# Last mixer in pairs of heads: two-head queries on row halves of the array, means on GpSimd, output blocks between transposes

## The chip, the cores and the metric

One core of a Trainium2 chip runs the whole program, one launch. The metric is the time on the device in microseconds; a time of the kernel is the median of its runs.

## The reference, cut to what matters

Two transformer stacks of two layers each, on 256 latent and 256 context tokens of width 1024, follow each other. The change lies in the fourth and last mixer, an mLSTM with 8 heads (64 query and key columns, 128 value columns per head), run in both directions (r = 0, 1) over the latents, from a state that the context left:

```python
def body(carry, inp):
    c_mat, n_vec, m = carry
    qc, kc, vc, ic, fc = inp
    b = jnp.cumsum(fc, axis=-1)
    logd = b[..., :, None] - b[..., None, :] + ic[..., None, :]
    logd = jnp.where(tri, logd, -jnp.inf)
    inter = b + m[..., None]
    m_t = jnp.maximum(inter, jnp.max(logd, axis=-1))
    s = jnp.einsum('bhtd,bhsd->bhts', qc, kc) * jnp.exp(logd - m_t[..., None])
    w_inter = jnp.exp(inter - m_t)
    num = einsum('bhts,bhsv->bhtv', s, vc) + w_inter[..., None] * einsum('bhtd,bhdv->bhtv', qc, c_mat)
    den = jnp.sum(s, axis=-1) + w_inter * einsum('bhtd,bhd->bht', qc, n_vec)
    out = num / jnp.maximum(jnp.abs(den), jnp.exp(-m_t))[..., None]

def _mlstm_readout(h, o, norm_w, w_out):      # h: sum over both directions
    h = h * lax.rsqrt(jnp.mean(h * h, axis=-1, keepdims=True) + EPS)
    return (jax.nn.sigmoid(o) * (h.reshape(...) * norm_w)) @ w_out
```

After it come the norm, the gate and the residual, and the last MLP (1024 to 4096 to 1024).

## The kernel before

Each engine has its own program, written out by hand in order; they meet on semaphores. Weights stream from HBM by SyncE into a ring of four raw tiles (`raw`). A walk over the blocks (`walk.take`) splits each block of 128x1024 into a high part by ScalarE (L1747, `split`) and a low part by VectorE (L2482) or, where `low_by_pool` is set, by GpSimd (L3486), up to five blocks ahead. TensorE then makes every product of the projections from three fp32r matmuls (high by high, high by low, low by high: L764, L770, L771; `mm3`). Products inside the mixer (`mm`, L774) are plain fp32, each of them two TensorE instructions in the trace. Eight PSUM banks are handed out in order of return (`ps.take`, `ps.give`).

Between the blocks the walk also drops units of the modulation product: multiply-adds of `ada` tiles on VectorE (L2507), so many per block by the table `RATE`. The last piece of a chunk of gates closes with a high copy (ScalarE), a low remainder `accl` (VectorE, L2550), two matmuls with ones (TensorE) and two operations that make the gate rows `G` (L2564, L2566). `walk.ensure` forces what is still open.

The last mixer (`mlstm` in all four engines' programs) goes over 16 steps, `steps = (h, r)`, both directions of head 0, then of head 1 and so on. Step j of TensorE: `maxima` of the next step (selects the row of maxima, into `mD`), for r = 0 `matches(h)` (keys by queries, both blocks of keys, into `mS`), one `gate_part` or `key_part` (12 fp32r matmuls of a projection that fills the step), then `back` of the step before: two matmuls of the queries with the state `m_C` and three of the weighted scores `m_S` with the values `m_vl`. The keys of heads 2p and 2p+1 lie in rows 0 to 63 and 64 to 127 of one tile; the queries have one tile per head, of which the other 64 rows are zero (GpSimd memsets), so each product runs over 128 rows. VectorE: `front` (decay arguments, L3297), `weigh` (scores by decays, L3307), `back` (adds up numerator and denominator, L3318), `over_den` (three small operations, L3327 to L3331), `head_sum` (both directions added, L3337, twice), and for each pair of heads `means` (L3344), `normed` (L3350), `gated` (L3362, twice), `gated_low` (L3370). ScalarE: the exponentials (`front`, L2364, twice), `back` (state part scaled, `m_T`, L2373, twice), `over_den` (L2381), `head_squares` (L1779), `o_out`, `gated_high` (L2397). GpSimd: `root` (power -1/2, L3699), `gate` (L3704) and the low parts of the weight blocks. Decay, score and state tiles are chosen by the direction r, two of each.

Each pair of heads is turned by four transposes (`normed` of TensorE, L1624) at steps 8 and 12, and after the loop. Then `proj_last` multiplies by `ml_w_out`: four blocks (all 1024 rows) for output columns 0 to 511 of both token tiles, `walk.ensure((3, 2))` for the gates of this layer, then four more blocks for columns 512 to 1023, tile 2 and then tile 3. In `transition` each tile is squared, gated (`gated_out`, L2681), added to the residual, normed and transposed for the MLP.

## Time and profile before

| | us |
|---|---|
| median of 3 runs | 1907.23 (1904.70 to 1908.61) |
| the profiled execution, its own time | 1903.66 |
| its span, first to last instruction | 1901.8 |
| mean granted TensorE clock | 0.997 |
| TensorE busy | 1862.8 (98%) |
| VectorE busy | 1374.1 (72%) |
| ScalarE busy | 926.8 (49%) |
| GpSimd busy | 248.4 (13%) |
| chain that ended last | TensorE 85%, VectorE 7%, ScalarE 3% |

TensorE carries nearly the whole span, so over most of it only its own instructions count; where it is idle, the chain of waits passes to another engine. The times of the trace are counted from the start of the span. Matmuls overlap in the trace, so what one costs is read from start to start.

### The profile page before, as it was taken

What the parts mean: (1) busy time and instruction counts of PE and PEld (TensorE: products, weight loads), DVE (VectorE), ACT (ScalarE), POOL (GpSimd) and SP (SyncE); (2) the same over time, 40 slices, a digit from 0 to 9 for tenths busy, and PEclk for the clock granted to TensorE, in tenths of its full rate; (3) what the DMA queues carried; (4) which work ended last, traced back from release to release, by engine and by line L of the source; (5) the groups of instructions that cost most, each with busy time, mean ns of one, the idle gap of its engine ahead of it and who ended that gap; (6) DMA issues with size and microseconds to landing.
All of it is one profiled execution on the core that took longest, in us unless ns stands there. A gap on an engine that the chain in (4) does not pass through costs nothing.

```text
span 1901.8 us, 27100 instructions
## 1 busy us (share of the span) xinstructions
PE 1862.8 (98%) x10121; PEld 1578.6 (83%) x10121; DVE 1374.1 (72%) x2135; ACT 926.8 (49%) x1593; POOL 248.4 (13%) x331
## 2 busy tenths in 40 slices
PE   7999999999999999999999999999999999989998
PEld 3878888888888788899998889888888878878997
DVE  5898778878766565789987766777665477676765
ACT  3666463424144473666552236433424354656654
POOL 1111011111111202201110001010110020321000
PEclk9999999999999999999999999999999999999999
DMA  9544255656652641588854433555554255237763
GB/s 317 153 126 144 78 177 178 209 176 192 189 188 59 200 130 53 175 270 281 268 179 145 139 104 112 177 178 169 174 168 141 60 183 169 86 108 248 224 191 112
DMA packets 192433, 315.31 MB, mean 166 GB/s; under 512 B 16229, under 2 KB 113840, under 8 KB 192304
## 3 DMA queue, kind: packets, MB, share of 16 engines
q1 hardware_dynamic: 163024, 210.09, 34.4%
q0 software_dynamic: 29280, 103.51, 18.0%
q8 instruction: 81, 1.33, 0.3%
q14 instruction: 48, 0.39, 0.1%
HBM read 312.50 MB, written 1.05 MB: 165 GB/s over the span
## 4 chain that ended last, share of the span: by engine, by line
PE 85%; DVE 7%; ACT 3%; issue 3%; DMA 1%; POOL 1%; DVEq 0%; SPq 0%; POOLq 0%; ACTq 0%
PE bank L764 26%; PE bank L771 24%; PE bank L770 24%; PE bank L774 6%; PE bank L769 2%; PE bank L767 2%; DVE acc L2507 1%; DVE w L2482 1%; PE bank L826 1%; PE bank L850 1%; ACT junk L1779 1%; POOL st L3558 1%; DMA raw<-in_ada_w 1%; DVE X L2626 1%; DVE HL L2611 0%
## 5 line engine op out<-in xcount | busy, mean ns | idle before, releaser
L1747 ACT ACTIVATE w<-raw 128x1024 fp32r<-128x1024 f32 (+2 forms) x386 | 398.3, 1040 | 527.7 <-PE bank L771 464.7
L2482 DVE TENSOR_TENSOR w<-raw,w 128x1024 fp32r<-128x1024 f32 (+3 forms) x368 | 438.8, 1201 | 223.0 <-ACT w L1747 222.5
L764 PE MATMUL bank<-HH,w 128*128 128x256 f32 (+1 forms) x1552 | 508.5, 328 | 3.4 <-DVE HH L2609 2.0
L770 PE MATMUL bank<-HL,w 128*128 128x512 f32 (+1 forms) x1232 | 412.5, 335 | 0.0
L771 PE MATMUL bank<-HH,w 128*128 128x512 f32 (+1 forms) x1232 | 412.4, 335 | 0.0
L2507 DVE SCALAR_TENSOR_TENSOR acc<-ada,sc,acc 128x512 f32<-128x512 f32 x518 | 362.6, 748 | 2.3
L764 PEld LDWEIGHTS bank<-HH,w 128*128 128x128 f32 x1552 | 291.4, 188 | 30.3 <-issue 4.4
L764 PE MATMUL bank<-w,UH 128*128 128x512 f32 x768 | 300.6, 391 | 0.0
L771 PE MATMUL bank<-w,UL 128*128 128x512 f32 x768 | 299.1, 389 | 0.0
L770 PE MATMUL bank<-w,UH 128*128 128x512 f32 x768 | 298.9, 389 | 0.0
L771 PEld LDWEIGHTS bank<-HH,w 128*128 128x128 f32 x1232 | 230.5, 187 | 26.1
L770 PEld LDWEIGHTS bank<-HL,w 128*128 128x128 f32 x1232 | 230.7, 187 | 25.7 <-issue 0.2
L771 PEld LDWEIGHTS bank<-w,UL 128*128 128x128 f32 x768 | 144.2, 188 | 30.3
L770 PEld LDWEIGHTS bank<-w,UH 128*128 128x128 f32 x768 | 144.2, 188 | 29.2
L764 PEld LDWEIGHTS bank<-w,UH 128*128 128x128 f32 x768 | 144.2, 188 | 29.1
L3495 POOL DMA_DIRECT2D ada<-in_mod_w x96 | 69.4, 724 | 535.2 <-DVE acc L2507 535.2
L764 PE MATMUL bank<-w,HH 128*128 128x512 f32 (+2 forms) x336 | 128.2, 382 | 2.0 <-issue 2.0
L771 PE MATMUL bank<-w,HL 128*128 128x512 f32 (+2 forms) x336 | 126.7, 377 | 0.0
L770 PE MATMUL bank<-w,HH 128*128 128x512 f32 (+2 forms) x336 | 126.5, 376 | 0.0
L2784 DVE TENSOR_TENSOR UL<-tp,UH 128x256 fp32r<-128x256 f32 (+1 forms) x128 | 69.9, 557 | 76.4 <-ACT UH L1938 75.9
L3495 POOL DMA_DIRECT2D ada<-in_ada_w x80 | 58.0, 726 | 344.8 <-DVE acc L2507 344.8
L1930 ACT ACTIVATE ta<-bank 128x256 f32<-128x256 f32 (+1 forms) x128 | 62.5, 488 | 81.5 <-PE bank L771 78.4
(366 smaller groups left out, 2515.9 us busy)
## 6 DMA issues: line engine op xcount, KB each, us to landing
raw<-in_mlp_w SPq DMA_DIRECT2D x256, 512.0 KB, 4.4
ada<-in_mod_w POOLq DMA_DIRECT2D x96, 512.0 KB, 4.7
ada<-in_ada_w POOLq DMA_DIRECT2D x80, 512.0 KB, 4.6
raw<-in_ml_w_qkvo SPq DMA_DIRECT2D x28, 512.0 KB, 3.7
raw<-in_conv_w_in SPq DMA_DIRECT2D x24, 512.0 KB, 3.6
raw<-in_ada_w SPq DMA_DIRECT2D x12, 512.0 KB, 6.2
raw<-in_mla_w_o SPq DMA_DIRECT2D x8, 512.0 KB, 3.9
raw<-in_gla_w_v SPq DMA_DIRECT2D x8, 512.0 KB, 3.7
```

The lines of the kernel that those rows point to most:

```text
L764: pe.matmul(o, sh, mh, start=start, stop=False, skip_group_check=True)
L767: pe.matmul(o, sl, mh, start=False, stop=False, skip_group_check=True)
L769: return pe.matmul(o, sh, ml, start=False, stop=stop, skip_group_check=True)
L770: pe.matmul(o, sh, ml, start=False, stop=False, skip_group_check=True)
L771: return pe.matmul(o, sl, mh, start=False, stop=stop, skip_group_check=True)
L774: return pe.matmul(o, st, mv, start=start, stop=stop, skip_group_check=True)
L1747: act.activation(k.halves(n)[0], k.raw[(NDIRECT + n) % NRAW][:, 0:m], ACT.Copy).then_inc(*k.w_hi.up("w hi", n))
L1930: act.activation(t1[:, 0:N], b[:, 0:N], ACT.Relu).then_inc(*b.emptied())
L2482: dve.tensor_tensor(low, k.raw[(NDIRECT + n) % NRAW][:, 0:m], high.bitcast(F32), ALU.subtract).then_inc(*k.w_lo.up("w lo", n))
L2507: i = dve.scalar_tensor_tensor(out=o, in0=k.ada[m % NADA][:, q, :], scalar=cc, in1=o, op0=ALU.mult, op1=ALU.add)
L2784: dve.tensor_tensor(UL[:, n, 0:N], t2[:, 0:N], UH[:, n, 0:N].bitcast(F32), ALU.subtract).then_inc(*k.u_lo.up("u lo", li, q, n))
L3495: pool.dma_start(k.ada[m % NADA][:], src).then_inc(*k.ada_in[m % NADA].up("ada in", m, by=16))
```

## The change

Steps of the loop are now pairs: `(0,0) (1,0) (0,1) (1,1) (2,0) ...`. The query tile holds a pair of heads (four tiles, no zeros, two memsets and half the copies gone). `matches` runs once per pair and `recalled` (the queries with the state) once per pair and direction, with 64-row operands that alternate between the two row halves of the array and write two banks. Decay, score and state tiles are chosen by the head's parity. ScalarE scales both heads' state parts at the odd steps. Sums, squares and transposes of a pair stand one to two steps later. The mean moves from VectorE to GpSimd, just ahead of the power. `ml_w_out` is streamed as rows 0 to 511 for both column halves, then rows 512 to 1023. Its first four blocks come right after the loop, the transposes of heads 4, 5 and of 6, 7 stand ahead of the third and the fourth of them, and the last four blocks close tile 2 and then tile 3 (`gated_out` of columns 0 to 511 now per tile). `RATE` of the last layer's first part goes from 0.8 to 0.9.

```diff
-    yield from tokw(A["ml_w_out_2"][0], 0, D, 0, D)
+    for r0 in (0, D // 2):
+        yield from tokw(A["ml_w_out_2"][0], r0, D // 2, 0, D)
-RATE = [(1.2, 1.05), (0.65, 0.45), (0.4, 0.8), (0.8, 0.35)]
+RATE = [(1.2, 1.05), (0.65, 0.45), (0.4, 0.8), (0.9, 0.35)]
...
-        def matches(h):
...
-                p = mm(b[:, s * 256:s * 256 + 256], k.mkT[:, pr, s * 128:s * 128 + 128], k.mqT[:, h, :])
+        def matches(pr):
+            bs = [ps.take("mS", 2 * pr + i) for i in range(2)]
...
+            for s in range(2):
+                for i, b in enumerate(bs):
+                    w.wait_ge(*b.before())
+                    c = i * 64
+                    p = mm(b[:, s * 256:s * 256 + 256], k.mkT[c:c + 64, pr, s * 128:s * 128 + 128], k.mqT[c:c + 64, pr, :])
...
+        def recalled(pr, r):
+            bs = [ps.take("mx", 2 * pr + i, r) for i in range(2)]
+            w.wait_ge(*ps.of("mC", r, pr // 2).is_empty())
+            for t in range(2):
+                for i, b in enumerate(bs):
...
+                    p = mm(b[:, t * 129:t * 129 + 129], k.mqT[c:c + 64, pr, t * 128:t * 128 + 128], k.mC[c:c + 64, r, pr, :])
...
         def back(h, r):
-            b1, b2 = ps.take("mn", h, r), ps.take("mx", h, r)
+            if h % 2 == 0:
+                recalled(h // 2, r)
+            b1 = ps.take("mn", h, r)
...
-        steps = [(h, r) for h in range(8) for r in range(2)]
+        steps = [(2 * pr + i, r) for pr in range(4) for r in range(2) for i in range(2)]
...
-            if j in (8, 12):
-                turned = normed((j - 8) // 4)
+            if j in (10, 14):
+                turned = normed((j - 10) // 4)
...
-        proj_last(("y", 3, 2), (k.mOH, k.mOL), [2, 3], o_ready, 2, among={2: lambda: ps.give(normed(3))})
+        for nh in range(2):
+            bs = [ps.take("y", 3, 2, nh, t) for t in (2, 3)]
+            for kk in range(2):
+                if nh * 2 + kk == 2:
+                    ps.give(normed(2))
+                if nh * 2 + kk == 3:
+                    ps.give(normed(3))
+                n = walk.take()
...
+        walk.ensure((3, 2))
+        slots = walk.take4()
+        for t in (2, 3):
+            for nh in range(2):
+                for kk in (2, 3):
+                    p = part(kk, nh, t, slots[nh * 2 + kk - 2])
...
-            act.activation(k.mqT[0:64, 2 * n, :], b[0:64, 0:256], ACT.Copy, scale=0.125)
-            act.activation(k.mqT[64:128, 2 * n + 1, :], b[64:128, 0:256], ACT.Copy, scale=0.125).then_inc(*b.emptied())
+            act.activation(k.mqT[:, n, :], b[:, 0:256], ACT.Copy, scale=0.125).then_inc(*b.emptied())
...
+            if c % 2:
+                back(j - 1)
+                back(j)
...
         def root(fp):
...
-            w.wait_ge(*at("mean", "mz", fp))
+            w.wait_ge(*at("mz sq", fp * 2 + 1))
+            pool.tensor_scalar(s[1], s[0], 1.0 / 128, EPS, ALU.mult, ALU.add).then_inc(*own.up())
+            w.wait_ge(*own.last())
```

How it moves instructions. Line numbers in the rows of the changed kernel are its own. TensorE, in the loop, before (`m_C,m_qT`: queries with state; `m_vl,m_S`: scores with values; `m_M,Gh`: maxima; `m_qT,m_kT`: matches; the row after them is the filling projection):

```order
L774 MATMUL bank<-m_C,m_qT 128x129 x2
L774 MATMUL bank<-m_vl,m_S 128x129 x3
L774 MATMUL bank<-m_M,Gh 128x256
L774 MATMUL bank<-m_qT,m_kT 128x256 x2
L764 MATMUL bank<-HH,w 128x256
```

The same place now:

```order
L775 MATMUL bank<-m_C,m_qT 128x129 x4
L775 MATMUL bank<-m_vl,m_S 128x129 x3
L775 MATMUL bank<-m_M,Gh 128x256
L775 MATMUL bank<-m_qT,m_kT 128x256 x4
L765 MATMUL bank<-HH,w 128x256
```

The queries stand there four at a time, in every second step, the matches four at a time, in every fourth; there are as many of them in all as before.

ScalarE, four steps late in the loop, before (`m_D`: exponentials; `m_T`: state parts; `Y<-Y`: division by the denominator; `junk,Y<-Y`: squares; `w<-raw`: high part of a weight block):

```order
L2364 ACTIVATE m_D<-m_D,m_cols 128x256 x2
L2373 ACTIVATE m_T<-bank,m_cols 128x129 x2
L2381 ACTIVATE Y<-Y 128x128 x2
L1779 ACTIVATE junk,Y<-Y 128x128 x2
L2364 ACTIVATE m_D<-m_D,m_cols 128x256 x2
L2373 ACTIVATE m_T<-bank,m_cols 128x129 x2
L2393 ACTIVATE m_so<-bank 128x256
L1747 ACTIVATE w<-raw 128x1024
```

and now:

```order
L2408 ACTIVATE m_D<-m_D,m_cols 128x256 x2
L2438 ACTIVATE m_so<-bank 128x256
L2418 ACTIVATE m_T<-bank,m_cols 128x129 x4
L2426 ACTIVATE Y<-Y 128x128 x2
L2408 ACTIVATE m_D<-m_D,m_cols 128x256 x2
L1823 ACTIVATE junk,Y<-Y 128x128 x2
L1791 ACTIVATE w<-raw 128x1024
L2408 ACTIVATE m_D<-m_D,m_cols 128x256 x2
```

The state parts of two steps follow each other, and the step between has none.

VectorE, behind the loop, before (`HL<-tp,HH`: low part of the mixer's last heads; `accl`: low remainder of the gate sums):

```order
L3370 TENSOR_TENSOR HL<-tp,HH 128x2x256
L2482 TENSOR_TENSOR w<-raw,w 128x1024 x4
L2550 TENSOR_TENSOR accl<-acc,Gh 128x512
L2564 TENSOR_TENSOR G<-bank,gb 128x512
L2566 SCALAR_TENSOR_TENSOR G<-G,gb 128x512
```

and now:

```order
L3425 TENSOR_TENSOR HL<-tp,HH 128x2x256
L2538 TENSOR_TENSOR w<-raw,w 128x1024 x4
L2620 TENSOR_TENSOR G<-bank,gb 128x512
L2622 SCALAR_TENSOR_TENSOR G<-G,gb 128x512
L2538 TENSOR_TENSOR w<-raw,w 128x1024
```

`accl` is gone from here; it now stands ahead of the loop.

## Rows read from the trace of the kernel before

**Rows 1.** Windows: busy us (x instructions), granted clock, DMA share, GB/s.
```profile
1621.70:1643.60 21.90, 21.90 (x179) 21.48 (x179) 13.06 (x34) 16.29 (x45) 8.10 (x6) 1.00 0.30 97
1643.60:1675.80 32.20, 26.55 (x206) 24.57 (x204) 22.84 (x54) 22.37 (x66) 11.46 (x7) 1.00 0.20 66
1675.80:1697.40 21.60, 16.82 (x80) 14.23 (x81) 16.13 (x23) 11.09 (x26) 7.07 (x6) 0.92 0.29 88
1697.40:1708.70 11.30, 11.11 (x50) 8.86 (x48) 7.84 (x13) 4.88 (x10) 1.12 (x2) 1.00 0.52 162
```

**Rows 2.** Waits of TensorE, 1621 to 1725 us: total, times, longest.
```profile
PE bank L1624 <- DVE Y L3350: 6.2, 3, 2.6
PE bank L774 <- DVE accl L2550: 2.2, 1, 2.2
```

**Rows 3.** Timeline of TensorE in one step: start, us, instructions.
```profile
1621.76 0.61 PE L774 MATMUL bank<-m_C,m_qT 128*128 128x129 f32 x4
1622.20 0.83 PE L774 MATMUL bank<-m_vl,m_S 128*128 128x129 f32 x6
...
1622.99 1.03 PE L774 MATMUL bank<-m_qT,m_kT 128*128 128x256 f32 x4
1623.67 0.47 PE L764 MATMUL bank<-HH,w 128*128 128x256 f32 x1
```

**Rows 4.** Windows of tile g_s in an earlier mixer; last: the first one's group.
```profile
732.62:734.55 1.93, 1.92 (x16) 1.46 (x16) 0.04 (x1) 0.00 (x0) 1.00 0.00 0
734.55:736.47 1.92, 1.92 (x10) 1.44 (x8) 0.00 (x0) 0.00 (x0) 1.00 0.00 0
...
L774 PE MATMUL bank<-Y,g_s 64*128 64x256 f32 x16 | 2.0, 389 | 0.0
```

**Rows 5.** Timeline of VectorE in the loop; last two: groups, 1643.6 to 1675.8.
```profile
1641.33 0.69 DVE L3297 SCALAR_TENSOR_TENSOR m_D<-bank,m_msk 128x512 f32<-128x512 f32 x1
...
1644.09 1.45 DVE L3337 SCALAR_TENSOR_TENSOR Y<-Y 128x128 f32<-128x128 f32 x2
...
1652.35 0.62 DVE L3337 SCALAR_TENSOR_TENSOR Y<-Y 128x128 f32<-128x128 f32 x2 [0.35 <-ACT Y L2381]
...
1658.11 0.69 DVE L3297 SCALAR_TENSOR_TENSOR m_D<-bank,m_msk 128x512 f32<-128x512 f32 x1
...
L3318 DVE TENSOR_TENSOR Y<-bank,m_T 128x258 f32<-128x258 f32 x9 | 3.8, 426 | 8.7 <-ACT m_T L2373 8.7
...
L1779 ACT ACTIVATE junk<-Y 128x128 bf16<-128x128 f32 x8 | 2.5, 310 | 4.6 <-DVE Y L3337 4.5
```

**Rows 6.** Timeline of GpSimd in the loop.
```profile
1643.14 1.99 POOL L3486 TENSOR_TENSOR w<-raw,w 128x1024 fp32r<-128x1024 f32 x1
...
1674.53 1.38 POOL L3699 TENSOR_TENSOR Y<-Y,minus_half 128x4 f32<-128x4 f32 x1 [5.75 <-DVE Y L3344]
...
1676.48 2.37 POOL L3486 TENSOR_TENSOR w<-raw,w 128x1024 fp32r<-128x1024 f32 x1
```

**Rows 7.** Timeline of VectorE behind the loop and in the transition.
```profile
1674.96 0.68 DVE L3307 TENSOR_TENSOR m_S<-bank,m_D 128x512 f32<-128x512 f32 x1
...
1675.90 3.10 DVE L3337 SCALAR_TENSOR_TENSOR Y<-Y 128x128 f32<-128x128 f32 x2
...
1689.20 0.88 DVE L3362 SCALAR_TENSOR_TENSOR tp<-bank,m_nwc,m_so 128x256 f32<-128x256 f32 x2 [1.69 <-PE bank L1624]
1690.78 0.69 DVE L3370 TENSOR_TENSOR HL<-tp,HH 128x512 fp32r<-128x512 f32 x1 [0.70 <-ACT HH L2397]
1691.80 4.63 DVE L2482 TENSOR_TENSOR w<-raw,w 128x1024 fp32r<-128x1024 f32 x4 [0.33 <-ACT w L1747]
1696.35 0.68 DVE L2550 TENSOR_TENSOR accl<-acc,Gh 128x512 fp32r<-128x512 f32 x1
...
1709.27 0.21 DVE L2588 TENSOR_SCALAR st<-ysq 128x1 f32<-128x1 f32 x1 [0.33 <-ACT junk L1779]
1709.40 0.68 DVE L2681 TENSOR_TENSOR Y<-bank,G 128x512 f32<-128x512 f32 x1
```

More of the change, by code:

```diff
@@ L1633, in mlstm @@
                 maxima(*steps[j + 1])
-            if r == 0:
-                matches(h)
-            else:
+            if j % 4 == 0:
+                matches(h // 2)
+            if r == 1:
                 ps.give(ps.of("mS", h))
@@ L1906, in transition @@
         walk.cut_next()
+        if (li, part) == (3, 2):
+            y_out(li, part)(0, 3)
         y_out(li, part)(1, 3)
@@ L2758, in transition @@
         walk.ensure((nli, 3 * which), (nli, 3 * which + 1))
+        if (li, part) == (3, 2):
+            gated_out(li, part, 0, 3)
         y_out(li, part)(1, 3)
@@ L3289, in mlstm, with front @@
         proj_feat(1, kt_out)
-        def front(h, r):
+        def front(j):
+            h, r = steps[j]
             b = ps.of("mD", h, r)
@@ L3339, in head_sum @@
             a.then_inc(*k.z_dve.up("head sum", h))
-        def means(fp):
-            w.wait_ge(*at("mz sq", fp * 2 + 1))
-            ms = [k.st_ml[:, a, :].rearrange("p (t h) -> p t h", t=2)[:, :, fp * 2:fp * 2 + 2] for a in range(2)]
-            dve.tensor_scalar(ms[1], ms[0], 1.0 / 128, EPS, ALU.mult, ALU.add).then_inc(*k.mean_in.up("mean", "mz", fp))
         def normed(fp):
@@ L3373, in mlstm @@
         walk.low_by_pool = True
-        steps = [(h, r) for h in range(8) for r in range(2)]
-        front(*steps[0])
-        for j, (h, r) in enumerate(steps):
+        steps = [(2 * pr + i, r) for pr in range(4) for r in range(2) for i in range(2)]
+        front(0)
+        for j in range(16):
+            done, c = j // 4 * 2 - 2, j % 4
             if j < 15:
-                front(*steps[j + 1])
+                front(j + 1)
             if j < 2 or j % 2 == 0:
                 walk.take()
-            weigh(h, r)
+            weigh(j)
             if j == 1:
@@ L3386, in mlstm @@
                 back(*steps[j - 1])
-            if h and r:
-                head_sum(h - 1)
-            if h and not r:
-                over_den(h - 1)
-            if j in (6, 10, 14):
-                means((j - 6) // 4)
-            if j in (7, 11, 15):
-                normed((j - 7) // 4)
-            if j in (9, 13):
-                gated((j - 9) // 4)
-            if j in (10, 14):
-                gated_low((j - 10) // 4)
-        walk.take()
+            if c == 3:
+                over_den(done + 2)
+            if done >= 0 and c == 0:
+                over_den(done + 1)
+            if done >= 0 and c in (1, 2):
+                head_sum(done + c - 1)
+            if j in (9, 13):
+                normed((j - 9) // 4)
+            if j in (11, 15):
+                gated((j - 11) // 4)
+            if j == 13:
+                gated_low(0)
         back(*steps[-1])
         over_den(7)
+        head_sum(6)
+        gated_low(1)
+        normed(2)
         head_sum(7)
+        walk.take()
         gated(2)
-        means(3)
         gated_low(2)
@@ L3409, in mlstm @@
         walk.low_by_pool = False
-        proj_last(3, 2, [2, 3])
+        for _ in range(4):
+            walk.take()
+        walk.ensure((3, 2))
+        walk.take4()
+        gated_out(3, 2, 0, 2)
     w.wait_ge(*at("ident"))
@@ L3707, in mlstm @@
         for j in range(16):
-            if j in (6, 10, 14):
-                root((j - 6) // 4)
-                gate((j - 6) // 4)
+            if j in (8, 12):
+                root((j - 8) // 4)
+                gate((j - 8) // 4)
             if j < 2 or j % 2 == 0:
                 walk.take()
-        walk.take()
+        root(2)
+        gate(2)
         gate(3)
         root(3)
+        walk.take()
         walk.low_by_pool = False
```

129 lines of the change are left out of this document (75 added, 54 removed).

## Prediction

> **What bounds the kernel now.** I read the page first: TensorE is busy for 98% of the span and holds 85% of the chain that ended last. So a change can win only where TensorE is idle, slow, or does work that falls away. The windows [rows 1] split the stretch that the change touches in four. In 1621.7 to 1643.6 (`back` of steps 0 to 7) TensorE is busy throughout: it is the bound. In 1643.6 to 1675.8 (up to the last `back`) it is busy 26.55 of 32.2 us. In 1675.8 to 1697.4 (the last filling product, the first half of the output product) it is busy 16.82 of 21.6 us, at a granted clock of 0.92. In 1697.4 to 1708.7 (the second half) it is full again. Idle sums to 5.65 + 4.78 = 10.4 us; the clock took 8% of 21.6 us, 1.7 us. The waits of TensorE [rows 2] name two causes: 6.2 us of three waits by the transposes for `normed` of VectorE, and 2.2 us of the gate's matmul for `accl`. The last two windows hold what can be had; all of it, with the work that falls away below, would be 14 us.
>
> **Row halves.** TensorE's pieces are read from start to start [rows 3]. The state part of one step is 1622.20 - 1621.76 = 0.44 us. Matches of one head are 1623.67 - 1622.99 = 0.68 us, and the matmul behind them shows 0.47 us where those that follow it show 0.28, so 0.87 us. Are two row halves really at work at once? An earlier mixer alternates 64-row products in the same way [rows 4]: 16 of them, all of the form 64*128 with 256 columns, lie within 1.93 us, and in the next 1.92 us only the 8 with 128 rows (the other two counted are tails). Eight slots, of 128 rows or of a pair, take the same time; if one is the 0.87 / 4 = 0.216 us of a match (the trace shows four instructions for a head), eight make 1.73 us, so 0.2 us goes with each change of shape, and 0.4 us with a visit there and back. The Trainium skill (TensorEngine Tiling (Array Packing), Key Properties) says that changing the tiling mode drains TensorE; the row agrees and gives the price. Now per pair of heads: matches before 2 x 0.87 = 1.74 us, after 0.87 + 0.4 = 1.27 us. State parts, per pair and direction: before 0.88, after 0.44 + 0.4 = 0.84 us. So four pairs save 4 x (0.47 + 0.08) = 2.2 us of TensorE's work, and where it is the bound (7 of 16 steps) 2.2 x 7/16, **1.0 us**.
>
> **The late loop.** Here the bound is VectorE's order of work with its round trips to ScalarE. Its first instruction of a step starts at 1641.33 and, four steps later, at 1658.11 [rows 5]: 16.8 us, where TensorE needs 12.5 to 13 us (21.9 us for seven steps, [rows 1], and 0.44 us of transposes). In each step VectorE waits for `m_T` before its `back`: 8.7 us in nine steps, 0.96 us each. The state part on ScalarE stands behind an exponential that itself waited for VectorE. In the changed order both state parts of a pair are made at the odd steps, so that at the even ones they are there: 2 x 0.96 us less. `head_sum` stands a step behind its ScalarE division: the 0.35 us that it waited, twice. The mean (0.14 us) is GpSimd's. Together 1.92 + 0.70 + 0.14 = 2.8 us. Then GpSimd: two `head_sum` operations take 0.62 us at 1652.35, and 1.45 us at 1644.09, where a low part on GpSimd runs from 1643.14 to 1645.13 [rows 5, 6]; they end just behind it. The same thing takes 3.10 us at 1675.90 [rows 7], under low part 1676.48 to 1678.85. The Trainium skill (GPSIMD Engine Reference, in its table and again among its limits) says that GpSimd shares its SBUF interfaces with VectorE, with contention when a VectorE instruction has two SBUF inputs; `head_sum` has, `back` and `weigh` read one from PSUM and keep their 0.43 and 0.68 us throughout, so the trace agrees. In the new order the mean, power and gate of a pair start half a step earlier against the `head_sum` that follows, but the queue is longer by the mean, so I let the 0.83 us go and put 0.7 us of such waits in again. Four steps come to 16.8 - 2.8 - 0.1 = 13.9 us, eight to 27.8 us where they took 32.2; I add 1.1 us for two places where I expect more: ScalarE makes `o_out` ahead of the state parts in one odd step of four, and `matches` of the last pair takes the bank that a state part just left. That is **3.3 us** less.
>
> **Behind the loop.** I measure from the end of the last `weigh` (1674.96 + 0.68 = 1675.65, [rows 7]) to the last matmul of the output, 1708.35 (the end of `accl`, 1697.03, and the 11.3 us of the last window): 32.7 us. After: the last `back` and filling product end by 2.1 us (a step of 21.9 / 7 = 3.1 us without maxima, state part and matches). The three output blocks that come ahead of the last transposes take 2.78 us each (11.11 us for four blocks, [rows 1]), with one set of transposes 0.44 us: TensorE reaches the last transposes at 10.9 us. VectorE's chain up to the last `head_sum`: two `back` (0.43 each), two sets of denominators (three small operations each, none longer than the 0.21 us of the one at 1709.27, [rows 7]: 0.6), `gated` 0.88, two `head_sum` (0.62), a low part 0.69, `normed` 0.68, and 0.7 us of round trips, 6.2 us in all. Behind it: squares (two of 0.31 us [rows 5] with their sums, 0.8), the mean, the power 1.38 [rows 6] and `normed` 0.68. The mean on GpSimd has no row: it lies between 0.14 us (what VectorE took) and 1.38 us (the power on the same four elements), and is nearest to the power, an operation of that engine and shape; I take 1.0 us; at either end what it costs is under 1 us. That is 10.9 us, and with a low part of 2.37 us on GpSimd beside it that holds up VectorE for part of its time, `normed` comes at 11.6 us, so transposes end at 12.1 us. From `gated` to the last low part were 1691.47 - 1689.20 = 2.3 us [rows 7]: 14.4 us. Now the gain: before, TensorE could not begin the second half until **four** low parts of weights (4.63 us) and `accl` (0.68 us) stood behind that point on VectorE. `accl` is ahead of the loop now, so only the first low part (0.2 + 1.2 us) is needed: 15.8 us. The other three come every 1.16 us, and TensorE takes 2.78 / 2 = 1.39 us for each half block, so they are hidden. Then 48 matmuls, 10.9 us (11.11 in [rows 1] with the gate's own): end at 26.7 us, **6.0 us** less, the lower clock's 1.7 us included, since no wait of 2.6 us is left in a row.
>
> **Transition.** `gated_out` of columns 0 to 511 of tile 3 (0.68 us) now lies in VectorE's order ahead of the last tile's mean, where before it idled 0.33 us [rows 7]: **0.35 us more**. It waits there for nothing later than its squares, but the tile's mean and gating are queued behind it.
>
> **At nothing:** the memsets and halved query copies lie beside full TensorE windows. So do the `ada` units that the rate 0.9 brings forward; if VectorE were late there, TensorE would wait. The stream of `ml_w_out` has the same blocks in another order; the DMA share in these windows is 0.2 to 0.52.
>
> **Sum:** -1.0 - 3.3 - 6.0 + 0.35 = -9.95 us, against the profiled execution's 1903.66 us: 1893.7 us. That execution lay 3.6 us under the median, so against 1907.2 us I predict 1897.3 us. Some 0.2% (3.8 us) is what a measurement of this kernel can tell from no change.
>
> **Rivals.** (1) *GpSimd holds VectorE* (slower). The longer GpSimd queue (mean, power, gate, then 2.37 us of low part) falls upon both `head_sum` pairs of each of three late pairs. For: rows 5 to 7 show it twice. Against: the one at 1652.35 was free, and in most steps GpSimd has nothing to do (11.46 of 32.2 us busy, [rows 1]). Price: up to 2.4 us per place, six places, 14.4 us: 4.5 us slower than before. It decides for slower when the added waits pass 9.9 us, that is at five of six places. Chance 0.04. (2) *Halves do not overlap* in this place: TensorE's pieces stay at 1.74 and 0.88 us and 12 visits x 0.4 us = 4.8 us come on top; against my sum that is 1.0 + 4.8 x 7/16 = 3.1 us in the early steps and about 0.6 us late, -6.2 us in all. Rows 4 speak against it. 0.08. (3) *The late loop keeps its pace*: the wait for `m_T` only moves to the odd steps, where two state parts and `o_out` stand ahead. -1.0 - 6.0 + 0.35 = -6.6 us. For: ScalarE was busy 22.37 of 32.2 us there [rows 1]. 0.16. (4) *The tail keeps its wait*, because something else stands last before the second half (the last pair's chain late by 4 to 5 us, through GpSimd's power); of the 6.0 us only 1 us of the clock's stays: -1.0 - 3.3 + 0.35 - 1.0 = -4.9 us. 0.12. (5) *Both 3 and 4*: -1.0 + 0.35 - 1.0 = -1.6 us, no change that can be told. 0.09. (6) *It does not do what it says*: the order of instructions shows the pairs, so this is only that `accl` is late all the same; it is within 4.
>
> The forecast has 0.51. Faster by over 0.2%: forecast, 2, 3 and 4, 0.87, less 0.02 for their low ends; within 0.2%: 0.11; slower: 0.04. The range: best case all idle and clock regained, 14 us less 0.35, is 1893.6 us; at the other end case 4 with its spread, 1904 us.
>
> **What would show it.** Right: TensorE's wait for `normed` at the transposes under 2 us in all instead of 6.2; no wait for `accl`; matches with 64-row operands, 8 in about 0.9 us; starts of VectorE's steps 14 us apart per four; the granted clock at 1.0 between the loop and the second half; `m_T` waits of VectorE in every second step only. Wrong: `head_sum` of 2 to 3 us under low parts on GpSimd; new waits of TensorE for ScalarE or for banks ahead of `matches`; a second half that starts over 18 us behind the last `weigh`; a loop where four steps still take over 16 us.

## The result, and the profile after

| | before | after |
|---|---|---|
| median, us | 1906.21 (1904.70 to 1908.61, 4 runs) | 1892.90 (1891.75 to 1893.16, 4 runs) |
| ratio | | 0.9928, 95% interval 0.9911 to 0.9945 |
| the profiled execution | 1903.66 | 1892.93 |
| its span | 1901.8 | 1891.1 |
| TensorE busy | 1862.8 | 1858.7 |
| VectorE busy | 1374.1 | 1370.1 |

The changed kernel is faster by 0.72%, 13.3 us between the medians and 10.7 us between the two profiled executions. The interval of the ratio stands for 10.5 to 17.0 us. The fourth run of before, made beside the changed kernel, moved its median from 1907.23 to 1906.21.

Where is it? I cut both traces at the same five marks of TensorE's program: the first product of `matches`, the first score product (`m_vl,m_S`) of the 8th and of the 16th `back`, the first product of the second half of the output projection, and the transposes of the last tile in the transition. The stretches are called **early**, **late**, **tail** and **second half** from here on. Windows, columns as in rows 1 (length, busy us of TensorE, its weight loads, VectorE, ScalarE and GpSimd with instructions, granted clock, DMA share, GB/s). Before:

```profile
1615.20:1644.11 28.91, 28.91 (x236) 28.39 (x235) 17.18 (x41) 20.46 (x54) 10.60 (x7) 1.00 0.34 106
1644.11:1676.31 32.20, 26.55 (x204) 24.57 (x203) 22.93 (x54) 21.91 (x64) 11.46 (x8) 1.00 0.20 66
1676.31:1697.42 21.11, 16.33 (x79) 13.72 (x77) 15.62 (x22) 11.11 (x26) 6.56 (x5) 0.92 0.29 91
1697.42:1714.02 16.60, 15.75 (x90) 13.28 (x89) 12.11 (x21) 7.78 (x16) 2.79 (x5) 1.00 0.46 142
```

The changed kernel:

```profile
1617.26:1645.41 28.15, 28.15 (x239) 25.75 (x239) 17.44 (x41) 20.08 (x54) 10.38 (x7) 1.00 0.29 92
1645.41:1670.69 25.28, 23.86 (x200) 21.62 (x199) 18.51 (x46) 20.00 (x60) 10.94 (x9) 1.00 0.27 85
1670.69:1687.59 16.90, 14.99 (x79) 11.97 (x77) 12.00 (x24) 9.27 (x25) 7.63 (x8) 1.00 0.20 62
1687.59:1704.48 16.89, 15.82 (x89) 13.36 (x89) 15.23 (x24) 10.79 (x22) 2.79 (x5) 1.00 0.60 189
```

Early -0.76, late -6.92, tail -4.21, second half +0.29: 98.82 us became 87.22, **11.6 us less**. Two differences lie outside and are not the change's. The first mark itself is 2.06 us later; 1.94 of that is there at 1574 us and 1.77 at the start of the first mixer, 78.76 us before against 80.53, in code that the change does not touch. The granted clock shows where it comes from: from 47.4 to 50.8 us it is 0.50 in the profile of the changed kernel (13 matmuls) and 1.00 in that of before (21 matmuls). In the 14 profiles of this study the first mark lies between 1615.2 and 1616.3 us in the four without such a stretch ahead of it, and between 1617.0 and 1618.6 in the ten with one or two. And from the last mark to the end it is 187.8 us before and 186.6 after, because before ran with a granted clock of 0.50 from 1718.0 to 1720.0. That differs from one execution to the next too: of the 14 profiles 7 have the long ending (187.6 to 188.2 us) and 7 the short one (186.6 to 186.7), and the last two experiments, equal in the stretch, differ in it.

Waits of TensorE in the changed kernel, 1617 to 1710 us, against [rows 2]:

```profile
PE bank L1635 <- DVE Y L3405: 2.4, 2, 1.3
PE bank L851 <- DVE Y L2655: 1.1, 2, 0.9
...
PE bank L765 <- ACT w L1791: 0.8, 1, 0.8
```

The transposes wait 2.4 us for `normed` instead of 6.2, nobody waits for `accl`, and a new wait of 0.8 us for the first weights of the second half has come. The pieces of TensorE in one pair's step, timeline, against [rows 3]:

```profile
1629.47 0.72 PE L775 MATMUL bank<-m_C,m_qT 64*128 64x129 f32 x8
1630.11 0.94 PE L775 MATMUL bank<-m_vl,m_S 128*128 128x129 f32 x6
1630.80 0.36 PE L775 MATMUL bank<-m_M,Gh 128*128 128x256 f32 x1
1631.10 1.13 PE L775 MATMUL bank<-m_qT,m_kT 64*128 64x256 f32 x8
1632.16 0.39 PE L765 MATMUL bank<-HH,w 128*128 128x256 f32 x1
1632.39 0.29 PE L771 MATMUL bank<-HL,w 128*128 128x256 f32 x1
...
1655.26 1.86 PE L775 MATMUL bank<-m_qT,m_kT 64*128 64x256 f32 x8
1657.05 0.39 PE L765 MATMUL bank<-HH,w 128*128 128x256 f32 x1
```

Eight matches of a pair take 1632.16 - 1631.10 = 1.06 us from start to start and eight state products 0.64 us. That is not yet the price: the products around such a group start later too. The same place in the changed kernel with 128-row products (the experiment `e3_full_rows` below):

```profile
1631.67 0.37 PE L775 MATMUL bank<-m_M,Gh 128*128 128x256 f32 x1
1631.87 1.89 PE L775 MATMUL bank<-m_qT,m_kT 128*128 128x256 f32 x8
...
1633.72 0.28 PE L771 MATMUL bank<-HL,w 128*128 128x256 f32 x1
```

From the product ahead of the matches to the second one behind them it is 2.05 us there and 1.59 us here, 0.46 us less per pair. The state products with what surrounds them (from the last L772 ahead of them to `m_M`) take 1.59 us there and 1.54 here, 0.05 us less per visit. In the last pair the same eight matches take 1.79 us with no idle time shown in front of them: two of the eight instructions run at once, the other six come from 1655.99 on, behind the second of ScalarE's pieces of state part (1655.59 to 1655.94), which frees the bank of the second head. A wait in the middle of a group does not appear as one.

The groups of VectorE in the late stretch (busy us, mean ns, idle time before them and its releaser). Before:

```profile
L3337 DVE SCALAR_TENSOR_TENSOR Y<-Y 128x128 f32<-128x128 f32 x9 | 5.0, 588 | 0.9 <-ACT Y L2381 0.7
...
L3318 DVE TENSOR_TENSOR Y<-bank,m_T 128x258 f32<-128x258 f32 x8 | 3.4, 426 | 7.8 <-ACT m_T L2373 7.8
L3362 DVE SCALAR_TENSOR_TENSOR tp<-bank,m_nwc,m_so 128x256 f32<-128x256 f32 x4 | 1.7, 478 | 0.0
L3370 DVE TENSOR_TENSOR HL<-tp,HH 128x512 fp32r<-128x512 f32 x2 | 1.4, 684 | 0.0
...
L3327 DVE SCALAR_TENSOR_TENSOR Y<-Y 128x4 f32<-128x4 f32 x4 | 0.7, 166 | 0.4
```

After:

```profile
L3378 DVE TENSOR_TENSOR Y<-bank,m_T 128x258 f32<-128x258 f32 x8 | 3.4, 423 | 6.3 <-ACT m_T L2418 6.0 <-PE bank L775 0.3
L3397 DVE SCALAR_TENSOR_TENSOR Y<-Y 128x128 f32<-128x128 f32 x8 | 2.7, 383 | 0.0
L3387 DVE SCALAR_TENSOR_TENSOR Y<-Y 128x4 f32<-128x4 f32 x4 | 2.4, 594 | 0.3
...
L3417 DVE SCALAR_TENSOR_TENSOR tp<-bank,m_nwc,m_so 128x256 f32<-128x256 f32 x2 | 0.9, 476 | 0.0
L3425 DVE TENSOR_TENSOR HL<-tp,HH 128x512 fp32r<-128x512 f32 x1 | 0.7, 678 | 0.0
```

`head_sum` (L3337, L3397) is shorter by 2.3 us (1.9 inside the cut, where one operation of before only begins), since GpSimd's low parts now mostly miss it, and its wait for ScalarE is gone (0.9). The same hold-up has moved to the first small operation of `over_den` (L3327, L3387): 0.7 became 2.4 us, but 1.47 of them are the operation at 1670.66, which runs in the tail, so inside the late stretch it is 0.4 us. The waits of `back` fell by 1.5 us only: every second one has gone, as forecast, and the others for `m_T` grew from mostly 0.96 us to between 1.18 and 2.20. And 1.5 us of work (two `gated` operations, one low part) now stand behind the loop.

VectorE behind the loop, timeline, against [rows 7]:

```profile
1668.34 0.68 DVE L3367 TENSOR_TENSOR m_S<-bank,m_D 128x512 f32<-128x512 f32 x1
...
1670.66 1.47 DVE L3387 SCALAR_TENSOR_TENSOR Y<-Y 128x4 f32<-128x4 f32 x1
...
1679.20 0.88 DVE L3417 SCALAR_TENSOR_TENSOR tp<-bank,m_nwc,m_so 128x256 f32<-128x256 f32 x2 [2.12 <-PE bank L1635]
1680.78 1.47 DVE L3425 TENSOR_TENSOR HL<-tp,HH 128x512 fp32r<-128x512 f32 x1 [0.70 <-ACT HH L2442]
1682.17 0.68 DVE L3405 TENSOR_TENSOR Y<-Y 128x512 f32<-128x512 f32 x1
1683.66 0.88 DVE L3417 SCALAR_TENSOR_TENSOR tp<-bank,m_nwc,m_so 128x256 f32<-128x256 f32 x2 [0.82 <-PE bank L1635]
1685.24 0.69 DVE L3425 TENSOR_TENSOR HL<-tp,HH 128x512 fp32r<-128x512 f32 x1 [0.70 <-ACT HH L2442]
```

GpSimd in the same time, against [rows 6]:

```profile
1669.73 2.38 POOL L3548 TENSOR_TENSOR w<-raw,w 128x1024 fp32r<-128x1024 f32 x1 [4.98 <-ACT w L1791]
1672.19 0.20 POOL L3757 TENSOR_SCALAR Y<-Y 128x4 f32<-128x4 f32 x1
...
1678.32 1.01 POOL L3759 TENSOR_TENSOR Y<-Y,minus_half 128x4 f32<-128x4 f32 x1
1679.30 2.40 POOL L3548 TENSOR_TENSOR w<-raw,w 128x1024 fp32r<-128x1024 f32 x1
```

The root that the last `normed` (L3405) needs is there at 1679.33, but `normed` starts at 1682.17: VectorE first made `gated` of pair 2, waited 0.70 us for ScalarE's high half, and its low part took 1.47 us, until GpSimd's low part had ended. The last low part ends 16.9 us behind the last `weigh`.

### The profile page after: what moved, and what is told of

Read it like the earlier page. It is cut to its first block, busy times and chain, and to the rows that moved or that the text cites. A ratio compares the mean times of both kernels' runs of the same rounds, so it can differ in the third digit from the quotient of the medians.

```text
span 1891.1 us, 27083 instructions
## 1 busy us (share of the span) xinstructions
PE 1858.7 (98%) x10121; PEld 1571.5 (83%) x10121; DVE 1370.1 (72%) x2131; ACT 924.1 (49%) x1589; POOL 246.6 (13%) x333
## 4 chain that ended last, share of the span: by engine, by line
PE 87%; DVE 6%; ACT 3%; issue 2%; DMA 1%; POOL 1%; SPq 0%; DVEq 0%; POOLq 0%; ACTq 0%
PE bank L765 26%; PE bank L772 24%; PE bank L771 24%; PE bank L775 6%; PE bank L770 2%; PE bank L768 2%; DVE acc L2563 1%; PE bank L827 1%; DVE w L2538 1%; PE bank L851 1%; ACT junk L1823 1%; POOL st L3620 1%; DMA raw<-in_ada_w 1%; DVE X L2682 1%; DVE HL L2667 0%
## 5 line engine op out<-in xcount | busy, mean ns | idle before, releaser
L772 PE MATMUL bank<-HH,w 128*128 128x512 f32 (+1 forms) x1232 | 411.9, 334 | 0.0
L772 PE MATMUL bank<-w,UL 128*128 128x512 f32 x768 | 299.1, 389 | 0.0
L772 PEld LDWEIGHTS bank<-HH,w 128*128 128x128 f32 x1232 | 230.0, 187 | 25.9
L772 PEld LDWEIGHTS bank<-w,UL 128*128 128x128 f32 x768 | 144.2, 188 | 30.3
L772 PE MATMUL bank<-w,HL 128*128 128x512 f32 (+2 forms) x336 | 127.3, 379 | 0.0
```

Of the source, the lines that this page charges most:

```text
L772: return pe.matmul(o, sl, mh, start=False, stop=stop, skip_group_check=True)
```

## The experiments

There are twelve; the name in brackets is the one by which the expectations speak of them. Times are medians; ratios are against runs of the kernel before on the same chip. The stretches are read from each profile at the same marks.

### Putting it together part by part

**Rate alone** (`e2_before_rate09`). The kernel before with one number changed.

```diff
-RATE = [(1.2, 1.05), (0.65, 0.45), (0.4, 0.8), (0.8, 0.35)]
+RATE = [(1.2, 1.05), (0.65, 0.45), (0.4, 0.8), (0.9, 0.35)]
```

> The kernel before with the rate 0.9 alone. Theory A: TensorE ends the first half at 1694.9 and starts the second with its first low part instead of after accl (1697.42): 2.2 to 2.7 us less than before, the transposes' waits (6.2 us) unchanged. Theory B (the whole tail gain is the rate's, transposes and blocks count for nothing): 4 us or more less. Theory C (the rate is nothing without the new places of the output blocks): within 0.5 us of before.

1902.40 us, ratio 0.9979 (0.9970 to 0.9988). The tail went from 21.11 to 18.50 us, all else stayed: theory A, 2.6 us.

**Rate and places of the output blocks** (`e7_before_place`), the loop as before.

```diff
-    yield from tokw(A["ml_w_out_2"][0], 0, D, 0, D)
+    for r0 in (0, D // 2):
+        yield from tokw(A["ml_w_out_2"][0], r0, D // 2, 0, D)
...
-        ps.give(normed(2))
         gate_part(15)
...
+                if nh * 2 + kk == 2:
+                    ps.give(normed(2))
+                if nh * 2 + kk == 3:
+                    ps.give(normed(3))
```

> The kernel before with the rate 0.9 and the new places of the output blocks (two blocks, transposes of pair 2, a block, transposes of pair 3, a block), its loop in the old order with 128-row products. Theory A (the new places fill the waits behind the loop): the wait of 2.6 us for normed behind the last back is gone, normed of the last pair comes near 1687.7, the second half starts near 1692 against 1697.4 before: 5 to 6 us less than before, 2.5 to 3.5 less than with the rate alone. Theory B (the last low part bounds it either way): no more than 1 us less than with the rate alone.

1899.82 us, ratio 0.9964 (0.9952 to 0.9977). Tail 18.50 to 16.02, second half 16.56 to 17.12: 1.9 us less than with the rate alone in the stretch (2.6 by the medians), between theory A's 2.5 to 3.5 and theory B's 1. TensorE is busy 14.75 us in the tail against 15.90, so 1.15 of the 2.48 us are the granted clock (0.91 with the rate alone, 1.00 here). The second half grew by 0.56 us.

**Order by pairs** (`e14_full_mean`), with 128-row products and the means on VectorE. Against the changed kernel it is

```diff
-                    p = mm(b[:, s * 256:s * 256 + 256], k.mkT[c:c + 64, pr, s * 128:s * 128 + 128], k.mqT[c:c + 64, pr, :])
+                    p = mm(b[:, s * 256:s * 256 + 256], k.mkT[:, pr, s * 128:s * 128 + 128], k.mqT[:, 2 * pr + i, :])
...
+            if j in (8, 12):
+                means((j - 8) // 4)
```

> The changed kernel with 128-row products and the means on VectorE: of the loop only the order by pairs is left. It is to be set against the kernel before with rate and places (late half of the loop 32.2 us). Theory A (the order by pairs is the loop's gain, mean and halves are terms of their own that add up): early 29.8, late 26.1, tail 19.0 us, some 2 us slower than e8_mean_vector. Theory B (the parts lean on each other, so that without the mean on GpSimd and the halves the order by pairs is worth little): late above 28 us.

1898.09 us, ratio 0.9962 (0.9948 to 0.9975). Early 29.80, late 26.40, tail 18.26, second half 17.04: theory A, and what it asked of the loop came to 0.3 us. The sum is 1.5 us above the kernel with the means on VectorE below. The early stretch grew by 0.89 us, but only because the cut now holds the matches of six heads instead of five (0.87 us a head).

**Means on GpSimd as well, products still with 128 rows** (`e3_full_rows`). The first two lines of the diff above alone, with the same edit for the state products and the zeroed query tile.

> The changed kernel with 128-row matches and state products on zero-padded queries, in the new order of steps (only the row halves undone). Theory A (halves run at once and the loop is bound by TensorE nearly throughout now): the 16 match products cost 4 x 0.5 us and the state products 8 x 0.1 us more: 2.2 to 2.8 us slower than the changed kernel. Theory B (the loop is bound by VectorE and ScalarE in its late half, as I took it): about 1 us slower. Theory C (the halves do not overlap and only cost changes of shape): 1 us faster or more.

1896.30 us, ratio 0.9945 (0.9932 to 0.9957). Its stretches are 29.80, 25.28, 16.86 and 17.23:

```profile
1617.48:1647.28 29.80, 29.80 (x241) 29.18 (x240) 18.02 (x41) 20.80 (x56) 10.94 (x7) 1.00 0.30 89
1647.28:1672.56 25.28, 24.08 (x201) 23.20 (x200) 18.08 (x45) 19.66 (x60) 10.41 (x9) 1.00 0.27 84
```

Against the changed kernel +1.65 early and +0.00 late, 1.95 us in all (3.4 by the medians, with overlapping intervals of the ratios). That is under theory A's 2.2 and over theory B's 1. The early stretch, where TensorE is the bound, holds three visits of matches and four of state products: 3 x 0.46 + 4 x 0.05 = 1.6 us. In the late one the halves give nothing, though TensorE is idle for only 1.42 of its 25.28 us. So the late loop is not bound by TensorE, however full it looks.

Set one on the other, in us:

| kernel | early | late | tail | second half | sum | step |
|---|---|---|---|---|---|---|
| before | 28.91 | 32.20 | 21.11 | 16.60 | 98.82 | |
| + rate | 28.91 | 32.18 | 18.50 | 16.56 | 96.15 | -2.7 |
| + places | 28.91 | 32.18 | 16.02 | 17.12 | 94.23 | -1.9 |
| + pairs | 29.80 | 26.40 | 18.26 | 17.04 | 91.50 | -2.7 |
| + means on GpSimd | 29.80 | 25.28 | 16.86 | 17.23 | 89.17 | -2.3 |
| + row halves (after) | 28.15 | 25.28 | 16.90 | 16.89 | 87.22 | -2.0 |

### Taking one part away

**Rate back to 0.8 in the changed kernel** (`e1_rate08`).

> The changed kernel with the rate of the ada units back at 0.8; nothing else differs. Theory A (the rate's share is the low bias row accl getting out of the way of the four low parts of weights): VectorE makes accl behind the last low part of the pairs (1685.93 in the changed kernel) and the four low parts (0.33 + 4.63 + 0.68 us), so the second half of the output product starts near 1692 instead of 1687.6: 4 to 5 us slower than the changed kernel, up to 1 us more if the granted clock falls in the wait. Theory B (the rate is worth little, since the second half waits for its first low part anyway): within 1 us of the changed kernel.

1899.05 us, ratio 0.9964 (0.9950 to 0.9977). Theory A: the tail is 21.42 us (+4.5). Waits of TensorE, and the window of the second half:

```profile
PE bank L775 <- DVE accl L2606: 4.9, 1, 4.9
```

```profile
1691.13:1709.03 17.90, 16.87 (x91) 14.11 (x89) 12.12 (x21) 8.58 (x20) 2.79 (x5) 0.93 0.42 130
```

The wait of 4.9 us brings a lower granted clock behind it and another 1.0 us. The same number is worth 2.7 us in the kernel before and 5.9 in the changed one, where less else is in the way.

**Means back on VectorE** (`e8_mean_vector`).

```diff
-            pool.tensor_scalar(s[1], s[0], 1.0 / 128, EPS, ALU.mult, ALU.add).then_inc(*own.up())
...
+            dve.tensor_scalar(ms[1], ms[0], 1.0 / 128, EPS, ALU.mult, ALU.add).then_inc(*k.mean_in.up("mean", "mz", fp))
```

> The changed kernel with the four means made by VectorE again. Theory A (the mean costs 0.2 us wherever it stands; nobody waits for it): within 0.6 us of the changed kernel. Theory B (the mean on VectorE makes its queue wait for ScalarE's squares, and what stands behind it is late): 1 us or more slower, to be seen as idle time of VectorE before the mean. Theory C (the hand-over to GpSimd costs): 0.5 us or more faster.

1897.72 us, ratio 0.9950 (0.9937 to 0.9962). Stretches 28.16, 26.08, 18.96, 16.77: 2.7 us more. Theory B, and stronger than it said. VectorE and GpSimd, timelines:

```profile
1678.23 1.10 DVE L3410 TENSOR_TENSOR Y<-Y 128x512 f32<-128x512 f32 x1 [1.12 <-POOL Y L3766]
...
1682.78 2.48 DVE L3430 TENSOR_TENSOR HL<-tp,HH 128x512 fp32r<-128x512 f32 x1 [0.70 <-ACT HH L2442]
1685.18 0.68 DVE L3410 TENSOR_TENSOR Y<-Y 128x512 f32<-128x512 f32 x1
```

```profile
1677.19 1.01 POOL L3766 TENSOR_TENSOR Y<-Y,minus_half 128x4 f32<-128x4 f32 x1 [3.49 <-DVE Y L3404]
...
1682.35 2.36 POOL L3557 TENSOR_TENSOR w<-raw,w 128x1024 fp32r<-128x1024 f32 x1
```

GpSimd was idle 3.49 us for a mean of 0.17 us that stood in VectorE's queue behind `head_sum` and a low part. The power came late, VectorE then waited 1.12 us for it, and what follows fell upon GpSimd's low part (2.48 us for 0.69). The transposes waited 2.63 us in a row and the granted clock of the tail is 0.91, 1.3 of its 2.1 us.

**One state part per step on ScalarE again** (`e11_late_state`).

```diff
-            if c % 2:
-                back(j - 1)
-                back(j)
+            if j:
+                back(j - 1)
```

> The changed kernel with ScalarE making one state part in every step, as the kernel before did, instead of both of a pair at the odd steps; TensorE's pairs of products are unchanged. Theory A (the late loop gained because at the even steps m_T is there when VectorE comes to it): the late half of the loop (25.3 us in the changed kernel) gets half or more of its 6 us back, 3 us or more slower, with waits of VectorE for m_T in every step. Theory B (the gain is in the order of pairs itself, two VectorE chains in turn, and not in where ScalarE makes the state parts): under 1 us slower.

1899.89 us, ratio 0.9968 (0.9956 to 0.9981). Early 30.18, late 28.76, tail 15.80, second half 17.16: 4.7 us more: theory A's number, with 2.0 us in the early stretch where I expected none. Waits of TensorE:

```profile
PE bank L765 <- ACT m_T L2418: 3.5, 3, 1.9
PE bank L775 <- ACT m_T L2418: 2.7, 2, 1.4
```

It waits 6.2 us for banks that the second state part of a pair still holds, and VectorE's own waits ahead of `back` end at TensorE (10.8 us, 8 times) more than at `m_T` (7.5 us, 7 times). This run therefore does not price VectorE's waits by themselves: a pair made at once on TensorE has to be drained at once on ScalarE. What in the order by pairs brings its gain is not taken apart further by any run.

### What was left of the waits

**Order of VectorE and ScalarE behind the loop** (`e4_order`).

```diff
         gated(2)
-        gated_low(2)
         normed(3)
+        gated_low(2)
         gated(3)
...
-        for fp in range(2, 4):
-            gated_high(fp)
-        walk.low_by_pool = False
-        for _ in range(4):
-            walk.take()
+        gated_high(2)
+        walk.low_by_pool = False
+        walk.take()
+        gated_high(3)
+        for _ in range(3):
+            walk.take()
```

> The changed kernel with two moves behind the loop: VectorE makes normed of the last pair right behind gated of pair 2, while ScalarE makes the high half, and ScalarE splits the first weight block of the second half ahead of the high half of the last pair. Theory A (what stands last before the second half is VectorE's order): the transposes of the last pair no longer wait (1.08 us in the changed kernel), gated_low of the last pair ends near 1684.8 and the second half starts 1.3 to 1.8 us earlier; the whole 1.3 to 1.8 us faster than the changed kernel. Theory B (the second half waits for something else, its raw weights or the low part on GpSimd): under 0.5 us.

1892.42 us, ratio 0.9923 (0.9909 to 0.9936): in the runs not to be told from the changed kernel. In the trace the tail is 15.88 us, 1.0 less, between the theories. The reason is in two rows, VectorE and GpSimd:

```profile
1680.22 2.28 DVE L3406 TENSOR_TENSOR Y<-Y 128x512 f32<-128x512 f32 x1
```

```profile
1679.53 2.42 POOL L3549 TENSOR_TENSOR w<-raw,w 128x1024 fp32r<-128x1024 f32 x1
```

`normed`, 0.68 us elsewhere, took 2.28, until GpSimd was done. The hold-up goes to whatever SBUF operation VectorE has next.

**That low part on VectorE, all else as in the changed kernel** (`e5_low_vector`). `walk.low_by_pool = False` before the last `walk.take()` of the tail instead of behind it.

> The changed kernel with the last low part before the second half made by VectorE instead of GpSimd. Theory A (GpSimd holds VectorE only where both work on SBUF at once, and what it holds is not much more than what VectorE would spend itself): gated_low of pair 2 falls from 1.47 to 0.69 us, but VectorE pays 1.2 us for the low part, a part of it in its idle 2.1 us; the whole within 0.6 us of the changed kernel. Theory B (the contention is what made the chain behind the loop 2.5 us late against my working): 1 us or more faster.

1893.47 us, ratio 0.9927 (0.9915 to 0.9940); tail 17.04 us. `gated_low` is back at 0.69 us, and VectorE spent 1.23 us on the low part: theory A, no gain.

**Both, and `normed` in the loop ahead of the wait for `m_T`** (`e10_order_loop_low`).

```diff
             weigh(j)
+            if j in (9, 13):
+                normed((j - 9) // 4)
             if j:
                 back(*steps[j - 1])
```

> The two moves of e4_order, the low part on VectorE as in e5_low_vector, and in the loop normed of pairs 0 and 1 ahead of VectorE's wait for m_T instead of behind head_sum. Theory A (the loop is bound by TensorE but for the transposes of pair 1, which wait 1.30 us for a normed that could run in VectorE's 2.2 us of idle time): that wait goes as well, 2.5 to 3.2 us faster than the changed kernel, near 1890. Theory B (the wait only moves to the next product of the loop, since ScalarE is late for m_T by as much): 1.3 to 1.8 us faster, as e4_order.

1891.84 us, ratio 0.9918 (0.9905 to 0.9932). The transposes of the loop no longer wait, and late is 24.16 us, 1.1 less; but the second output block now waits 0.94 us for `gated_low` of pair 1. 85.50 us in all, 1.7 less than the changed kernel (1.1 by the medians). That is theory B's number but not its mechanism: the loop did get shorter, by 1.1 us, and a part of the freed time came back as a new wait.

**Three more moves** (`e12_best`).

```diff
-        head_sum(6)
         gated_low(1)
+        head_sum(6)
         normed(2)
...
         gated(3)
+        walk.take()
         gated_low(3)
```

and the low part of step 14 on VectorE behind `weigh` of step 15, not on GpSimd.

> e10_order_loop_low with three more moves: the low part of step 14 on VectorE in its idle 1.2 us behind weigh of step 15 (GpSimd's low part held the first operation of over_den(6) for 1.47 us), gated_low of pair 1 ahead of head_sum(6) (the second output block waited 0.94 us for it), and the first low part of the second half ahead of gated_low of the last pair. Theory A (each of them stands on the path): the wait of 0.94 us goes, the second half starts 1 to 1.6 us earlier than in e10_order_loop_low, near 1890 to 1890.5 us. Theory B (TensorE's waits only change their place): within 0.5 us of e10_order_loop_low.

1890.48 us, ratio 0.9922 (0.9910 to 0.9935). Late and tail of its windows:

```profile
1646.00:1670.15 24.15, 23.57 (x201) 21.59 (x200) 19.79 (x45) 19.16 (x57) 9.96 (x8) 1.00 0.26 89
1670.15:1684.99 14.84, 14.57 (x79) 12.17 (x78) 12.51 (x27) 10.17 (x28) 3.83 (x6) 1.00 0.22 72
```

and the row of VectorE that took 1.47 us in the changed kernel:

```profile
1671.60 0.17 DVE L3391 SCALAR_TENSOR_TENSOR Y<-Y 128x4 f32<-128x4 f32 x1
```

Theory A: the second half begins 1.3 us earlier in the tail's count (16.14 to 14.84) and the sum is 83.89 us, 3.3 less than the changed kernel.

**Output blocks in the order of features** (`e13_best_kk`).

```diff
-    for r0 in (0, D // 2):
-        yield from tokw(A["ml_w_out_2"][0], r0, D // 2, 0, D)
+    for r0 in (0, D // 4):
+        yield from tokw(A["ml_w_out_2"][0], r0, D // 4, 0, D)
+    yield from tokw(A["ml_w_out_2"][0], D // 2, D // 2, 0, D)
...
```

> e12_best with the first four output blocks in the order of features instead of columns (both halves of the columns for features 0 to 255, then for 256 to 511), so that gated_low of pair 1 is needed one block later. Theory A: what is left of the wait of the second block goes, 0 to 0.5 us less than e12_best. Theory B (two more PSUM banks are held from the first block on, and the transposes of pair 2 wait for one): slower than e12_best by 0.5 us or more.

1890.12 us, ratio 0.9921 (0.9907 to 0.9934). Tail 14.83 and sum 83.87 us: the same as the one before it to 0.02 us: the low end of theory A and not theory B, so nothing was left to gain there.

The last two are the best of the study, 3.3 us shorter than the changed kernel in the stretch and 2.4 to 2.8 us by the medians. The intervals of the ratios overlap the changed kernel's; that they are faster rests on the traces, in which equal code gave equal early and late stretches within 0.1 us.

## Why the prediction was right or wrong

The direction, the places and most mechanisms were right; the time, 1892.9 us, lies 0.7 us below the low end of the range and 4.4 below 1897.3. The 4.4 us have three parts. The stretch gained 11.6 us where the sum said 9.95: 1.65. I laid the sum against 1907.2 us, the median of three runs, and the median of four was 1906.2 (later groups of 9 to 15 runs gave 1905.3, 1905.7 and 1906.7): 1.0. The other 1.7 us are what the medians differ by beyond the stretch, 13.3 against 11.6; they lie inside the interval of the ratio, and no run shows a cause. The step that failed for the range is that base: the 13.3 us are still less than the 13.65 (14 - 0.35) that its low end allowed, and laid against 1906.2 that end would have been 1892.6. The range held no part for the scatter of before. The half clock behind the transition, up to 1.6 us in an execution and there in the profile of before, was not in it either.

In the sum three terms were mis-sized: two gains were 1.0 and 2.7 us too small, one 2.0 us too large. That they cancel in part, so that the sum is only 1.65 us off, is luck. Measured by the part-by-part table, the row halves gave 1.95 us where I had 1.0, the loop without them 6.0 (61.1 to 55.1 us, early and late together) where I had 3.3, and all behind the loop without them 3.6 where I had 6.0 - 0.35 = 5.65.

**Row halves, -1.0.** Measured 1.95. The price per pair came out (0.46 us for matches and 0.05 per visit of state products, where I had 0.47 and 0.04), the number of pairs did not: I took 7 of 16 steps, but matches stand at the head of each pair's four steps, so three pairs of four fall where TensorE is the bound. The rest (0.3) is in the second half, with no cause shown. That late steps give nothing was right. Rival 2 is out.

**The late loop, -3.3.** Mis-sized, the largest error: 6.0 us, of which the pairs took 4.9 and the means 1.1. The mechanism was there, with `m_T` waits of VectorE in every second step only, but its pieces had other sizes. In the late stretch, which fell by 6.9 us: waits of `back` I had at 1.92 us per four steps, 3.8 in eight; they fell by 1.5, since the waits that stay got longer (2.20 us at 1663.89). The waits for the division went, 0.9 us, where 0.70 per four steps had been 1.4. I let 0.83 us of hold-ups go and put 0.7 back for four steps, 0.3 less in eight; inside the cut they fell by 1.5 (1.9 less on `head_sum`, 0.4 more on `over_den`). Then I added 1.1 us for two places: the bank of the last pair's matches was one, 0.7 us. What I had not counted as a gain of the loop is the 1.5 us of `gated` and low part that went behind it, though I charged it there. And the mean, 0.14 us in my sum as an instruction, is worth 2.3 to 2.7 us as a link, 1.1 or less of it here. These rows do not make up the whole 6.9 us; the rest is not followed. Rival 3 is out.

**Behind the loop, -6.0.** Measured 32.7 to 29.7 us on my count from the last `weigh` (1669.02) to the last matmul of the output (1698.36 + 0.39): 3.0. (The mark at the 16th `back` lies 1.0 us later behind that `weigh` than before, so by this count 1.0 us of the table's tail belongs to the loop.) The chain up to the last `head_sum` took 8.1 us instead of 6.2 (1677.09): `over_den` held for 1.3 us and a longer `head_sum` under GpSimd's gate. And a step is missing in it: `gated` and `gated_low` of pair 2 stand between the last `head_sum` and the last `normed`, 2.97 us with the wait for ScalarE and the hold-up. So the last low part came at 16.9 us, not 14.4, and the second half at 18.6, not 15.8, over the 18 us that I had named as a sign of being wrong. My adding was off too, the other way: 6.2 + 0.8 + 1.0 + 1.38 + 0.68 is 10.1 us and not the 10.9 written. That moving `gated_low` behind `normed` pays was shown (1.0 us with the hold-up still there). The part on `accl` was right in kind: its wait cost 2.6 us in the tail of the kernel before and 4.5 in the changed one, and no wait of 2.6 us in a row was left, with the clock at 1.00. The mean's instruction took 0.20 us, not 1.0, and the power 1.01, not 1.38.

**Transition, +0.35.** The second half's stretch grew by 0.29 us, near the forecast, but as a sum of other steps: +0.56 with the new places and -0.34 with the row halves. TensorE's wait ahead of the last tile's transposes went from 0.66 to 0.85 us. No run prices the moved `gated_out` by itself.

**Rivals 1 and 4.** GpSimd did hold VectorE, at five places from 1645 us on, but for 0.3 to 1.3 us each and not the 2.4 that the rival put on each. The Trainium skill (GPSIMD Engine Reference, Key points) speaks of contention when a VectorE instruction has two SBUF inputs. The traces agree: every operation held here (`head_sum`, the first of `over_den`, `normed`, the low parts) is of that kind, and `back`, `weigh` and `gated`, which read one input from PSUM, kept 0.43, 0.68 and 0.88 us. Rival 4 was half true: the tail kept 1.08 + 0.75 us of waits, and the transposes 2.4 us in all, over the 2 us of my sign of being right.

## What to carry to other kernels

Price a small operation by the round trip it stands in, not by its length: moving a mean of 0.2 us to the engine that needed its result next was worth 2.3 us with 128-row products and 2.7 with row halves (there 1.3 of it the clock), because it had stood in VectorE's queue and held up what came behind it. When a step moves between stages, book it in both (less here, more there), and write down the whole queue of the engine that carries the chain, in order, before adding it up: the step that I left out stood in it. And where two parts lean on the same wait, each is worth more once the other is gone, so a part's price depends on the order of the sum: the rate gave 2.7 us in the old kernel and 5.9 in the new.

## What the runs showed of the hardware

In these traces a VectorE operation with two SBUF inputs beside one of GpSimd's low parts was held until that ended, whatever its own size: 128x4 took 1.47 us instead of 0.17, 128x512 took 2.28 and 2.48 instead of 0.68. What the GpSimd operation lost is not shown. Its low parts took 1.99 to 2.01 us up to about 1650 us and 2.35 to 2.42 from 1655 on, with a held operation beside them or without: the 1.99 us of [rows 6] stand beside the 1.45 us of `head_sum`, and one of 2.38 at 1666.41 in the kernel before has none. The hold-up came beside GpSimd's gate as well, a 128x512 operation with one tensor input (`head_sum` of 0.97 us at 1676.12 beside the gate at 1675.85, which took 0.84 us there and 0.61 at 1658.53), but not beside a power in the kernel before: `gated_low` at 1686.10 took its 0.69 us while GpSimd was at the power from 1685.78 to 1686.79.

TensorE's rows show less than its slack. A group whose products wait in its middle is shown as busy (eight matches in 1.79 us instead of 1.06). And the 128-row products, longer by an estimated 0.46 + 4 x 0.05 = 0.66 us in the late stretch, raised the busy time there by only 0.22 us (23.86 to 24.08) and its 25.28 us not at all.

The granted clock fell to 0.50 at or behind a wait of TensorE of 2.6 us and more in four of five profiles (0.91 to 0.93 over the window) and not in the fifth (2.67 us, clock 1.00). Behind the transition, where the waits are 0.7 to 0.9 and 1.0 us, it did so in 7 of 14, as it did near 47 and 802 us in ten of 14. What decides between these stays open.
